# Two moves on TensorE in a decoder layer: the first RWKV solution ahead of half a memory quarter, an S5 read-out behind one

## What is computed

```python
proj = h @ w_in
u_s5, p_ml, p_rw, p_mb = split_cols(proj, (GW, ML_COLS, RW_COLS, MB_COLS))
y = concatenate([s5_mixer(u_s5, ...), mlstm_mixer(p_ml, ...), rwkv7_mixer(p_rw, ...), moba_mixer(p_mb, ...)])
y = rms_norm(y per group, mix_out_gain) @ w_out
q = (h @ wq);  kv = (mem_n @ wkv)          # cross-attention: kv does not depend on x
o = softmax(q k^T / 16) v @ wo
silu(h @ w_in[:, :D_FF]) * (h @ w_in[:, D_FF:]) @ w_out
```

## Time and profile before

| what | us |
|---|---|
| median of 3 runs | 512.62 (512.31 to 513.15) |
| profiled execution, own time | 512.91 |
| its span, first to last instruction | 511.0 |
| PE busy in it | 490.9 |
| mean granted clock | 0.996 |

### The profile page before, as it was taken

The page is one execution under the profiler, slowest core; times in us unless marked ns, Lnnn a source line. Parts: engine busy times, 40 slices in busy tenths (PEclk is TensorE's granted clock), DMA queues, the critical chain, the costliest instruction groups (busy, mean ns, idle before and its releaser), DMA issues.

```text
span 511.0 us, 8527 instructions
## 1 busy us (share of the span) xinstructions
PE 490.9 (96%) x3498; PEld 448.5 (88%) x3498; DVE 389.9 (76%) x469; ACT 259.0 (51%) x413; POOL 172.7 (34%) x101
## 2 busy tenths in 40 slices
PE   6999899999799989999999999999999999999995
PEld 3999698978698869888999989999999999988884
DVE  4898999998777876779656457699999999962224
ACT  5678782424332244668855657544444444433432
POOL 0004507498979240000000000254334433454360
PEclk9999999999999998999999999999999999999999
DMA  7894247102122012627455360274455555545502
GB/s 260 354 328 170 83 132 280 60 25 83 65 101 83 19 66 84 246 84 246 158 214 173 117 241 7 88 284 166 165 171 196 205 176 187 206 151 199 214 28 83
DMA packets 12691, 79.19 MB, mean 155 GB/s; under 512 B 1483, under 2 KB 2156, under 8 KB 4076
## 3 DMA queue, kind: packets, MB, share of 16 engines
q1 hardware_dynamic: 12652, 78.65, 43.2%
HBM read 76.80 MB, written 1.84 MB: 154 GB/s over the span
## 4 chain that ended last, share of the span: by engine, by line
PE 73%; DVE 14%; POOL 5%; ACT 4%; issue 2%; DMA 1%; DVEq 0%; SPq 0%; POOLq 0%; ACTq 0%
PE bank L392 72%; DVE we_rest L373 3%; POOL arena L1047 3%; POOL arena L1034 1%; DVE vx L1766 1%; DVE arena L1739 1%; DMA kx<-x_t 1%; DVE arena L1731 1%; DVE arena L1732 1%; ACT we_high L367 1%; DVE bank L1557 1%; ACT arena L1310 1%; DVE arena L1751 0%; DVE wk_rest L373 0%; DVE wm_rest L373 0%
## 5 line engine op out<-in xcount | busy, mean ns | idle before, releaser
L373 POOL TENSOR_TENSOR w_rest<-ring,w_high 128x1024 fp32r<-128x1024 f32 x20 | 48.5, 2424 | 198.2 <-ACT w_high L367 198.2
L392 PE MATMUL bank<-h_high,w_high 128*128 128x256 f32 x384 | 102.9, 283 | 0.0
L367 ACT ACTIVATE w_high<-ring 128x1024 fp32r<-128x1024 f32 x64 | 67.3, 1058 | 69.3 <-PE bank L392 69.2
L392 PE MATMUL bank<-h_rest,w_high 128*128 128x256 f32 x352 | 99.6, 283 | 0.0
L392 PE MATMUL bank<-h_high,w_rest 128*128 128x256 f32 x320 | 90.6, 283 | 0.0
L392 PEld LDWEIGHTS bank<-h_high,w_high 128*128 128x128 f32 x384 | 71.7, 192 | 0.5 <-issue 0.4
L373 DVE TENSOR_TENSOR w_rest<-ring,w_high 128x1024 fp32r<-128x1024 f32 x38 | 48.5, 1282 | 30.0 <-ACT w_high L367 29.9
L392 PEld LDWEIGHTS bank<-h_rest,w_high 128*128 128x128 f32 x352 | 67.6, 192 | 0.0
L392 PEld LDWEIGHTS bank<-h_high,w_rest 128*128 128x128 f32 x320 | 61.4, 192 | 0.0
L392 PE MATMUL bank<-arena 128*128 128x128 f32 (+7 forms) x496 | 58.4, 296 | 1.9 <-ACT arena L1093 0.7
L392 PEld LDWEIGHTS bank<-arena 128*128 128x128 f32 (+3 forms) x496 | 51.5, 178 | 8.2 <-issue 1.4
(11 more groups left out here) (343 smaller groups left out, 1271.2 us busy)
## 6 DMA issues: line engine op xcount, KB each, us to landing
ring<-weights SPq DMA_DIRECT2D x49, 1024.0 KB, 4.9
third_slot<-weights SPq DMA_DIRECT2D x15, 1024.0 KB, 4.9
gain<-gains SPq DMA_DIRECT2D x3, 512.0 KB, 6.0
cst<-consts SPq DMA_DIRECT2D x1, 1472.0 KB, 8.3
par<-params SPq DMA_DIRECT2D x1, 1168.0 KB, 11.6
kx<-x_t SPq DMA_DIRECT2D x2, 512.0 KB, 5.7
ring<-weights SPq DMA_DIRECT2D x2, 512.0 KB, 6.6
vx<-mem_t SPq DMA_DIRECT2D x1, 1024.0 KB, 11.0
```

Source lines behind the costliest of these rows:

```text
L367: nc.scalar.activation(split_half(i)[0], raw_half(i), ACT.Copy).then_inc(S["w_high"], 1)
L373: e.tensor_tensor(rest_, raw_half(i), high.bitcast(F32), ALU.subtract).then_inc(rest_done(i)[0], 1)
L392: return nc.tensor.matmul(out_, lhsT, rhs, start=start, stop=stop, skip_group_check=True)
```

## The change

Two pairs of neighbours on PE are swapped. The second S5 read-out goes behind the first memory quarter, and the first solution of RWKV goes ahead of the first half of the fourth memory quarter:

```diff
--- before.py
+++ after.py
@@ -712,8 +712,8 @@
             ml_qk(1, 0)
             level_p(4, 0, 4)
             level_p(4, 1, 6)
+            wkv(0, 1)
             s5_out(1, 3)
-            wkv(0, 1)
             level_x(4, 0)
             level_x(4, 1)
 
@@ -750,8 +750,8 @@
             level_x(6, 1)
 
             mb_scores(3, 5)
+            solve_u(0, 4)
             wkv(3, 1, (0,))
-            solve_u(0, 4)
             o = pe_open(pe, "S0", 4)
             moved(pe, "U0")
             moved(pe, "rw_bkt")
```

## The result

| | before | after |
|---|---|---|
| median of 20 runs each, us | 512.63 (510.67 to 513.47) | 513.43 (511.12 to 514.21) |
| profiled execution's own time, us | 512.91 | 513.19 |
| its span, us | 511.0 | 511.3 |

The ratio is 1.0017, interval 1.0009 to 1.0025: +0.9 us, 0.5 to 1.3. The forecast was 513.1 with +0.46 us.

A forecast was written before the change was run, and what follows sets the result against it. PE's stream and its few waits were taken to bound the kernel (PE at work 96% of the span). 1.85 + 1.49 - 1.39 - 1.49 = +0.46 us gave a median of 513.1 us, no change; 8-in-10 range 511.7 to 515.2.

The forecast's parts named there:

- The start of the quarter: Memory quarter 0 still starts at 134.77, held by ACT's wait for POOL; PE idles 4.72 us ahead of it.
- Term 1: Second read-out, moved behind memory quarter 0, costs as much as one set densely between other work: +1.85 us.
- Term 2: One fall of PE's clock behind the 4.72 us wait ahead of quarter 0: +1.49 us, bounds nothing and 2.98.
- Term 3: Solution ahead of half of quarter 3 shrinks PE's wait ahead of quarter 4 to 0.1 us: -1.39, bounds 0 and -1.5.
- Term 4: With that wait shrunk, the slow clock in quarter 4's first half goes: -1.49 us, bounds 0 and the whole 1.49.
- my first rival: Clock fall at 192 stays, at quarter 4's first half, or most executions had none: +1.95, 514.6 us; 20%.
- The chain to kx doesn't move: U's copy is early but something else holds ACT; Terms 3 and 4 are 0: +3.34, 516.0 us; 8%.
- the quarter really starts earlier: Memory quarter 0 starts at about 130.1, -2.7 us in place of Terms 1 and 2: 507.0 us; 3%.
- The long wait costs no clock: No clock fall behind the wait ahead of quarter 0; Term 2 is 0: -1.03, 511.6 us; 12%.

The follow-up runs named there:

- after_gate: Changed kernel with ACT's high part and DVE's rest for memory quarter 0's first half made ahead of ACT's wait on rotated_back: 510.02 us, ratio 0.9956.
- swap1_only: Kernel before with only the first swap, the second read-out behind memory quarter 0: 516.43 us, ratio 1.0078.
- before_again: Kernel before, unchanged, run once more for a second trace: 510.19 us, span 508.4.
- before_filled: Kernel before with two added matmuls of constants in the 1.89 us wait ahead of memory quarter 4: 510.91 us, ratio 0.9975.
- after_filled: Changed kernel with four added matmuls of constants in the 4.7 us wait ahead of memory quarter 0: 511.30 us, ratio 0.9983.
- gate_split_swap2: Changed kernel with quarter 0's first-half high part and rest ahead of the rotated_back wait, read-out between its halves, second swap kept: 509.56 us, ratio 0.9945.

## Why the prediction was right

The two profiled executions can be laid on each other, since each had exactly one slow spell within the change's reach.

| term | predicted | traces | how it is read |
|---|---|---|---|
| 1, read-out set densely | +1.85 | +1.85 | 143.91 - 142.06 |
| 2, clock behind the long wait | +1.49 | +1.60 | 142.06 - 134.63 = 7.43, against 140.60 - 134.77 = 5.83 |
| 3, wait ahead of quarter 4 | -1.39 | -1.55 | 193.87 - 143.91 = 49.96, against 192.11 - 140.60 = 51.51 |
| 4, clock behind that wait | -1.49 | -1.49 | 2.95 against 4.44 |
| sum | +0.46 | +0.41 | |

The first place starts 0.14 us earlier in the trace of after (134.63 against 134.77), which leaves +0.27 us, and the spans differ by 0.3. So the sum holds for these two executions. That it comes out near zero is four terms of 1.4 to 1.9 us against each other; the single swaps, +4.0 and -3.1 us, test the two halves of it apart.

**The start of the quarter.** It stayed where it was, as the wait ahead of ACT's high part said; moving that wait (after_gate) moved the start. This was the step on which the most hung, some 6 us: read from PE's own row alone, the quarter seems to wait for the read-out, and the swap seems to fill 2.1 us.

**Term 1.** Right to the hundredth, since the same piece of work was timed in the same setting, and not absorbed later: swap1_only shows the later waits at their old 0.56 and 1.89 us.

**Term 2.** Right in size, and there in three traces of three, where I had allowed for nothing. The first half takes 1.52 us longer; the other 0.08 lie between it and the read-out. The filled wait shows the cause. The bound of nothing came from the 2.15 us row, a wait less than half as long. The Trainium skill says that long idle gaps re-throttle TensorE (TensorE: Matmul & The Clock Gate, section "HAM oscillation — how this bites in real kernels"), and the three traces with the 4.7 us wait agree. It doesn't account for the shorter ones: a fall followed the wait of 1.89 us in two traces of three, and the one of 0.90 us in one of ten.

**Term 3.** Right, 0.16 us short, of which the bound had 0.1: PE's wait vanished altogether (193.87 is where PE gets by its own work). What I named as late next, the S5 read-out instead of the inverse sums, is what DVE's row of after shows, 0.47 us of waiting for PE at 188.36. One step was taken as unchanged and wasn't: from the GELU's argument to the kx copy it was 5.18 us before (186.32 to 191.50) and is 4.80 now (188.36 to 193.16). With the old step, and the 0.61 us from the copy's start to PE's (191.50 to 192.11), quarter 4 would have started at 194.15 and not at 193.87. That the wait is gone altogether is luck to that extent; why the step is shorter isn't shown.

**Term 4.** Right for the execution that was profiled. I took a spell that one trace shows as a property of the kernel, and before_again shows an execution with the same wait and no spell behind it. There the change would cost 1.5 us more by my sum. It was my first rival, given 20%, that held this part of the truth: some executions had no fall there to begin with.

**What is left of the median.** The forecast, +0.46, lies at the lower end of the interval, 0.5 to 1.3, and why the median is 0.4 us above it stays open. The missing spell isn't shown to be the reason: executions of the kernel before under 511 us are 5 of 65, too few to move a median, and before_filled's gain of 1.3 us says that most executions had the spell. The clocks of the runs point to the changed kernel. Its mean granted clock was 0.987 in 7 of the 20 runs, with a median of 513.7 us, while the other 13 have one of 513.2; in the 45 runs of the kernel before beside the experiments it was never under 0.992. So some executions of the changed kernel have a further low clock. Part of it can lie behind PE's last product, where it costs nothing, as in after_filled; no trace was taken of one of these, and the clocks of the 20 runs of the kernel before aren't on record, so place and price stay open.

**The other rivals.** "The chain to kx doesn't move" and "the quarter really starts earlier" fell with the first trace. "The long wait costs no clock" fell with its first half at 0.62, and after_filled gives the price.

## What to carry to other kernels

Before a piece of work is put ahead of a waiting one to fill its wait, look up what the piece itself waits for, on every engine of its chain: here both hung on one semaphore, and the swap only took the work out of the wait. A wait of the matrix engine that grows can cost twice, by the work that is pushed out of it (1.85 us here) and by the slow clock behind it (1.5 us), so a wait that can't be removed is better filled: that gave 1.7 us in one kernel and 1.3 in the other. And where a gain is missing after a gate is opened, look for the engine that used to be ready in time only because the others were late: without the move of POOL's mask the opened gate gave nothing beyond the second swap alone (ratios 0.9945 and 0.9939), with it about 2 us.

## What the runs showed of the hardware

Matmuls of constants in a 4.7 us wait, with no use for their result, made the kernel 1.7 us faster. The same kernel with the same waits had its slow spells at different places: at 192.9 us in one trace of before, at 115.5 in another; at 115.6 and 177.0 in one trace of gate_split_swap2 and none in the next. The one at 177.0 followed a wait of only 0.9 us, with small products (128x64, 64x128 and 32-column read-outs) around it, and the same wait had no spell behind it in the nine other traces of that order. And a slow spell may cost nothing, where PE goes on to wait for another engine anyway, as in before_again at 115.5 us. So a single trace tells what a spell costs, 1.5 us, but not whether the median has it.
